# One hybrid layer on one core: attention's small products gathered at one point of each step, with the turning and the value products one step later

## The chip, the cores and the metric

The kernel is one program on one core of a Trainium2 chip. TensorE (PE) multiplies, VectorE (DVE), ScalarE (ACT) and GpSimd (POOL) work on rows, SyncE (SP) and ScalarE issue transfers. The metric is the device time of one execution in microseconds (us), the median of the runs.

## The reference

A decoder layer for 1024 tokens of width 1024: RMS norm, one wide input projection, sliding-window attention (window 128, 16 query heads, 4 key/value heads, a sink logit per head), a chunked mLSTM, two gated branch projections, an output projection and a final norm. What matters here is attention:

```
scores = einsum('bnqkgd,bnskd->bnkgqs', qb, kw) * (ATTN_HEAD_DIM ** -0.5)
allowed = (rel >= 0) & (rel < WINDOW) & (k_pos >= 0)
scores = where(allowed, scores, -inf)
probs = softmax(concatenate([scores, sink]))[..., :-1]
out = einsum('bnkgqs,bnskd->bnqkgd', probs, vw)
branch_a = einsum('bte,ed->btd', attn * silu(a_z), w_branch_attn)
```

Tokens are in 8 blocks of 128 (`n`), and each block of queries sees its own and the previous block of keys.

## The kernel before

The input projection runs as pairs of output tiles. A pair is seven products of 12 dense matmuls each (`PRODUCT` = 12, `PAIR` = 84), with 512 columns each, in the order 1, 6, 2, 7, 4, 5, 3, by `pairs(i0, lo, hi)`; all of them are recorded at L1036. Each product needs the high and the low part of a weight tile in a ring. SP loads the raw tile, ACT makes the high part (L1396), POOL makes the low part and the sums of tiles (L799, L794). ACT copies bank A away (L1435), DVE adds the other banks up (L2091 to L2115).

Attention's small operations are put in between these dense matmuls by position. There are four attention steps, one for each key/value head (`g` = 0 to 3; "group" below), and in each of them 3 * PAIR = 252 dense matmuls run. `attention_at(n, half)` gives the position in these 252 at which the program of an engine turns to block step `n`:

```
LEAD, TAIL = 12, 12
return LEAD + (3 * PAIR - LEAD - TAIL) * (2 * n + half) // (2 * NB + 2)
```

PE, ACT and DVE each walk through the block steps in their own queue. PE runs dense matmuls up to a position with `more(position)`; ACT and DVE do what belongs to the products that ended before it with `retire(position)`. In block step n of a group:

- PE at the first point runs `scores(n)` (L1123, q times k of 64 rows, two products side by side), which waits until DVE has `max_ready` for n-1. At the second point, some 12 to 13 dense matmuls later, it runs the value products of block n-2 (L1165, L1167, 64 output columns, two side by side) and then turns the probabilities of block n-1 (L1172).
- ACT copies the scores (L1596), waits for the row maximum, and takes the exponentials (L1599, L1601). For the first three blocks it also copies the attention output to `u_early` (L1609).
- DVE: `combine` (L2191 or L2194, then L2197 to L2203) merges two blocks of scores and makes the maximum, `select` (L2222, L2224) masks the turned probabilities, `gate` (L2236) multiplies the output by the gate, `normalise` (L2208 to L2214) scales the probabilities by the inverse of their sum. `silu` is L2230, and L2262 applies the gate to the three early blocks (in block step 5 of the last group, in 8 of the others). The order is combine(n), select(n-1), gate(n-2), normalise(n).

After the last group, ACT and DVE wait until all of `u_scratch` is stored (L1632, L2278) before the mLSTM part starts, because the store's source lies where they write next. ACT then makes the first taps of the convolution (L1713), small tables, and then the high parts for the first mLSTM pair; POOL follows with the low parts. At the start, ACT waits for a store of the values, loads `v_head` for the first group (L1493), and then makes the high parts for the next pair.

Tile sizes, transfers and buffers are not touched by the change. `probs` has two buffers; scores share two PSUM banks, turned probabilities have one and the value products one.

Of the kernel before, what the change touches and what calls it, by code (L numbers as in the profile page):

```python
# [9 lines left out]
ACT = mybir.ActivationFunctionType  # L10
# [3 lines left out]
P = 128  # L14
# [3 lines left out]
NB = T // P  # L18
# [36 lines left out]
PAIR = 7 * PRODUCT  # L55
# [1 line left out]
OPAIRS = NB // 2  # L57
BANK_A, BANK_B, BANK_C, BANK_D = 2, 3, 0, 1
EARLY = 3
LEAD, TAIL = 12, 12  # L60


def slot(t):
# [8 lines left out]
def until(eng, sem, value):  # L72

    if isinstance(value, int) and value <= 0:
        return
    eng.wait_ge(sem, value)
# [26 lines left out]

def attention_at(n, half):

    return LEAD + (3 * PAIR - LEAD - TAIL) * (2 * n + half) // (2 * NB + 2)


# [6 lines left out]
def build(nc, x, norm_w, w_in, b_in, sinks, conv_w, conv_b, mnorm_w, wba, wbm, w_out, fnorm_w, out):  # L115
    ctx = ExitStack()
    with ctx:
# [106 lines left out]
        u_early = at("u_early", M_AT, [P, 2, EARLY * P])  # L224
# [702 lines left out]
        def _(pe):  # L927
# [199 lines left out]
            def attention_step(g):  # L1127
                i0 = 1 + 3 * g
                done = [0]

                def more(hi):

                    pairs(i0, done[0], hi)
                    done[0] = hi

                for n in range(NB + 2):
                    more(attention_at(n, 0))
                    if n < NB:
                        if n == 0:
                            pe.wait_ge(k_in, 32 * (g + 1))  # L1140
                            pe.wait_ge(c11_out, i0)
                            pe.wait_ge(c12_out, i0)
                            if not later(g):
                                pe.wait_ge(g_ready, 1)
                        else:
                            pe.wait_ge(cur_copied, NB * g + n)
                            pe.wait_ge(max_ready, NB * g + n)
                        scores(n).then_inc(scores_done, 1)
                    if n <= NB:
                        more(attention_at(n, 1))  # L1150
                    if n >= 2:
                        m = n - 2
                        pe.wait_ge(pT_ready, NB * g + m + 1)
                        if m == 0:
                            pe.wait_ge(v_in, 16 * (g + 1))
                        if m == 0 and later(g):
                            pe.wait_ge(attn_gated, (NB - EARLY) * g)
                        if 1 <= m <= EARLY:
                            pe.wait_ge(attn_copied, EARLY * g + m)
                        if m > EARLY:  # L1160
                            pe.wait_ge(attn_gated, (NB - EARLY) * g + m - EARLY)
                        for r in range(2):
                            o = ps[64 * r:64 * r + 64, X[3], 0:2 * P]
                            heads = slice(2 * r, 2 * r + 2)
                            mm = nc.tensor.matmul(o, v_head[:, m, :], pT_cur[:, heads, :], start=True, stop=(m == 0))  # L1165
                            if m:
                                mm = nc.tensor.matmul(o, v_head[:, m - 1, :], pT_prev[:, heads, :], start=False, stop=True)  # L1167
                        mm.then_inc(pv_done, 1)
                    if 1 <= n <= NB:
                        pe.wait_ge(probs_ready, NB * g + n)  # L1170
                        for h in range(GR):
                            mm = nc.tensor.transpose(ps[:, X[2], h * P:(h + 1) * P], probs[(n - 1) % 2][:, h, :], ident[:])  # L1172
                        mm.then_inc(probs_turned, 1)
                more(3 * PAIR)

# [169 lines left out]
        def _(act):  # L1345
# [149 lines left out]
            def gate_tables():  # L1495
                act.wait_ge(g_turned, 1)
                A(gate_T[:].rearrange("p g h c -> p (g h c)"), ps[:, X[0], 0:2 * P], ACT.Copy).then_inc(g_ready, 1)

            def after(q, i, part, last=False):

                if q == 0:
                    keep_a(i, part)
                    high_4(i)
                if q == 1:
                    high_5(i)
                if q == 4 and not last:
                    high_1(i + 1)
                if q == 5 and not last:
                    high_6(i + 1)
                    high_2(i + 1)  # L1510
                if q == 6 and not last:
                    high_7(i + 1)
                    high_3(i + 1)
# [10 lines left out]
            act.drain()  # L1524
            load_k(0)
            gate_tables()
            act.wait_ge(v_out, 16 * 2)
            load_v(0)
            for q in range(2, 7):
                after(q, 0, None)  # L1530


            def attention_step(g):
# [33 lines left out]
                def retire(position):  # L1567

                    for q in range(done[0], position // PRODUCT):
                        if q < 7:  # L1570
                            after_z(q)
                        elif q < 14:
                            after_ga(q - 7)
                        else:
                            after_next(q - 14)
                    done[0] = max(done[0], position // PRODUCT)
# [9 lines left out]
                        act.wait_ge(z_used, 4 * g + m - 1)  # L1586
                    A(z_part[:, j, :], z_dest(j, h), ACT.Tanh, scale=0.5).then_inc(z_tanh, 1)

                for n in range(NB + 2):
                    retire(attention_at(n, 0))  # L1590
                    if n < NB:
                        pr = probs[n % 2]
                        act.wait_ge(scores_done, NB * g + n + 1)
                        if n >= 2:
                            act.wait_ge(probs_turned, NB * g + n - 1)
                        A(pr[:], both_blocks[:, :, 1, :], ACT.Copy).then_inc(cur_copied, 1)  # L1596
                        act.wait_ge(max_ready, NB * g + n + 1)
                        for h in range(GR):
                            A(pr[:, h, :], pr[:, h, :], ACT.Exp, scale=HD ** -0.5, bias=neg_max[:, h:h + 1],  # L1599
                              accum_out=row_sum[:, h:h + 1])  # L1600
                        A(sink_exp[:], sink_in[:], ACT.Exp).then_inc(exp_ready, 1)  # L1601
                    if n == NB and not final(g, KV):
                        load_k(g + 1)
                    if 2 <= n < EARLY + 2:
                        m = n - 2
                        act.wait_ge(pv_done, NB * g + m + 1)
                        if m == 0:
                            until(act, early_used, g)
                        A(u_early[:, :, m * P:(m + 1) * P], ps[:, X[3], 0:2 * P].rearrange("p (j n) -> p j n", j=2),  # L1609
                          ACT.Copy).then_inc(attn_copied, 1)  # L1610
                    if n <= NB:
                        retire(attention_at(n, 1))
                    if n in (3, 4):
                        for m in range(2):
                            tanh_z(2 * (n - 3) + m)
                    if n == (7 if final(g, KV) else 9):
                        act.wait_ge(u_half, g + 1)
                        act.dma_start(scr_u[ds(2 * g, 2)].rearrange("a p n -> p a n")[:, :, token_half(0)],
                                      silu_z[:, :, token_half(0)]).then_inc(u_half_out, 16)
# [373 lines left out]
        def _(dve):  # L1993
# [149 lines left out]
            def attention_step(g):  # L2143
# [91 lines left out]
                    z_m = silu_z[:, :, m * P:(m + 1) * P]  # L2235
                    return V.tensor_tensor(z_m, ps[:, X[3], 0:2 * P].rearrange("p (j n) -> p j n", j=2), z_m, ALU.mult)  # L2236

                for n in range(NB + 2):
                    retire(attention_at(n, 0))
                    if n < NB:  # L2240
                        combine(n)
                    if n <= NB:
                        retire(attention_at(n, 1))
                    if 1 <= n <= NB:
                        select(n - 1)
                    if n >= EARLY + 2:
                        gate(n - 2).then_inc(attn_gated, 1)
                    if n == NB + 1:
                        dve.drain()
                        dve.sem_inc(u_ready, 1)  # L2250
                    if n < NB:
                        normalise(n)
                    if n == 4:
                        silu(0)
                        silu(1)
                        dve.drain()
                    if n in (5, 7):
                        silu(2 if n == 5 else 3)
                        dve.drain()  # L2259
                    if n == (5 if final(g, KV) else 8):  # L2260
                        dve.wait_ge(attn_copied, EARLY * (g + 1))
                        V.tensor_tensor(silu_z[:, :, 0:EARLY * P], u_early[:], silu_z[:, :, 0:EARLY * P], ALU.mult)\  # L2262
                            .then_inc(early_used, 1)
                        dve.drain()
                        dve.sem_inc(u_half, 1)
# [403 lines left out]
```

## Time and the profile before

| | us |
|---|---|
| median of 3 runs | 1122.09 (1121.55 to 1122.24) |
| the profiled execution's own time | 1122.33 |
| span of the profiled execution | 1120.6 |

The profile is of one execution. Its span runs from the first to the last instruction; 1.7 us of the profiled time lie around it. The profiled time is 0.24 us above the median.

### The profile page before, as it was taken

What the parts mean: (1) busy time and instruction counts of PE and PEld (TensorE: products, weight loads), DVE (VectorE), ACT (ScalarE), POOL (GpSimd) and SP (SyncE); (2) the same over time, 40 slices, a digit from 0 to 9 for tenths busy, and PEclk for the clock granted to TensorE, in tenths of its full rate; (3) what the DMA queues carried; (4) which work ended last, traced back from release to release, by engine and by line L of the source; (5) the groups of instructions that cost most, each with busy time, mean ns of one, the idle gap of its engine ahead of it and who ended that gap; (6) DMA issues with size and microseconds to landing.
All of it is one profiled execution on the core that took longest, in us unless ns stands there. A gap on an engine that the chain in (4) does not pass through costs nothing.

```text
span 1120.6 us, 16419 instructions
## 1 busy us (share of the span) xinstructions
PE 1100.2 (98%) x5363; PEld 877.0 (78%) x5363; DVE 777.9 (69%) x1235; ACT 483.3 (43%) x1134; POOL 641.3 (57%) x441
## 2 busy tenths in 40 slices
PE   6999999999999999999999999999999999999997
PEld 5887777777777778888888888888887888788876
DVE  4966887887878887567756675669578312458897
ACT  7543443534434444454535364545455311131443
POOL 3577455465565469556955695659644434347440
PEclk9999999999999999999999999999999999999999
DMA  6244133142151141112311222122109433853423
GB/s 211 78 86 83 39 94 94 29 117 72 37 149 36 39 136 38 38 39 85 104 38 39 77 88 61 37 75 85 48 20 336 160 104 106 268 167 136 167 93 134
DMA packets 112804, 107.63 MB, mean 96 GB/s; under 512 B 7228, under 2 KB 96696, under 8 KB 111720
## 3 DMA queue, kind: packets, MB, share of 16 engines
q1 hardware_dynamic: 102760, 77.18, 23.2%
q10 hardware_dynamic: 9984, 29.69, 8.5%
q8 instruction: 33, 0.54, 0.2%
q14 instruction: 27, 0.22, 0.1%
HBM read 80.50 MB, written 26.35 MB: 95 GB/s over the span
## 4 chain that ended last, share of the span: by engine, by line
PE 79%; DVE 9%; ACT 4%; DVEq 3%; DMA 2%; issue 2%; ACTq 1%; SPq 0%; POOL 0%; POOLq 0%
PE ps L1036 50%; PE ps L1265 13%; PE ps L942 3%; PE ps L1123 2%; DMA w_raw<-in_w_branch_mlstm 1%; PE ps L1239 1%; PE ps L1223 1%; PE ps L1227 1%; PE ps L1236 1%; PE ps L1165 1%; DVE row_max L2197 1%; PE ps L1172 1%; DVEq L2259 1%; ACT ring_hi L1396 1%; DVE v L2427 1%
## 5 line engine op out<-in xcount | busy, mean ns | idle before, releaser
L799 POOL TENSOR_TENSOR ring_lo<-w,ring_hi 128x512 fp32r<-128x512 f32 x128 | 178.7, 1413 | 136.3 <-ACT ring_hi L1396 136.3
L799 POOL TENSOR_TENSOR ring_lo<-t,ring_hi 128x512 fp32r<-128x512 f32 x96 | 136.3, 1424 | 143.0 <-ACT ring_hi L1396 143.0
L1036 PE MATMUL ps<-s_hi,ring_hi 128*128 128x512 f32 x512 | 203.5, 397 | 0.0
L1036 PE MATMUL ps<-s_lo,ring_hi 128*128 128x512 f32 x512 | 202.6, 396 | 0.0
L1036 PE MATMUL ps<-s_hi,ring_lo 128*128 128x512 f32 x512 | 202.0, 395 | 0.0
L1036 PE MATMUL ps<-h_hi,ring_hi 128*128 128x512 f32 x384 | 152.1, 396 | 0.0
L1036 PE MATMUL ps<-h_hi,ring_lo 128*128 128x512 f32 x384 | 151.9, 396 | 0.0
L1036 PE MATMUL ps<-h_lo,ring_hi 128*128 128x512 f32 x384 | 151.4, 394 | 0.0
L1396 ACT ACTIVATE ring_hi<-w 128x512 fp32r<-128x512 f32 x128 | 75.6, 620 | 93.4 <-PE ps L1036 78.4
L1036 PEld LDWEIGHTS ps<-s_hi,ring_hi 128*128 128x128 f32 x512 | 96.2, 188 | 22.1 <-issue 3.0
L1036 PEld LDWEIGHTS ps<-s_hi,ring_lo 128*128 128x128 f32 x512 | 96.3, 188 | 21.8 <-issue 2.6
L1036 PEld LDWEIGHTS ps<-s_lo,ring_hi 128*128 128x128 f32 x512 | 96.3, 188 | 19.7 <-issue 1.3
L1599 ACT ACTIVATE probs<-probs,neg_max 128x128 f32<-128x128 f32 x128 | 49.9, 391 | 111.2 <-DVE neg_max L2203 111.2
L794 POOL TENSOR_TENSOR t<-w,t 128x512 f32<-128x512 f32 x64 | 94.4, 1475 | 5.1 <-issue 5.1
L782 POOL TENSOR_TENSOR w_hi<-w_raw,zero_col 128x1024 fp32r<-128x1024 f32 (+1 forms) x18 | 37.2, 2065 | 101.2 <-PE ps L1265 58.9
L1036 PEld LDWEIGHTS ps<-h_hi,ring_hi 128*128 128x128 f32 x384 | 72.2, 188 | 16.8 <-issue 1.3
L1036 PEld LDWEIGHTS ps<-h_hi,ring_lo 128*128 128x128 f32 x384 | 72.2, 188 | 15.4 <-issue 1.3
L1036 PEld LDWEIGHTS ps<-h_lo,ring_hi 128*128 128x128 f32 x384 | 72.2, 188 | 15.3 <-issue 1.3
L1396 ACT ACTIVATE ring_hi<-t 128x512 fp32r<-128x512 f32 x96 | 59.3, 623 | 53.8 <-PE ps L1036 46.6
L1265 PE MATMUL ps<-u_a,w_hi 128*128 128x512 f32 x256 | 79.1, 390 | 0.3 <-DVE u_a L2432 0.3
L1814 ACT ACTIVATE ev<-ev 128x1024 f32<-128x1024 f32 x16 | 17.0, 1062 | 110.5 <-DVE merged L2509 49.4
L1265 PE MATMUL ps<-u_m,w_hi 128*128 128x512 f32 x192 | 59.9, 393 | 0.4 <-POOL w_lo L784 0.4
(331 smaller groups left out, 2318.9 us busy)
## 6 DMA issues: line engine op xcount, KB each, us to landing
w<-in_w_in SPq DMA_DIRECT2D x128, 256.0 KB, 3.0
xs<-in_x SPq DMA_DIRECT2D x8, 512.0 KB, 8.3
ga_scratch<-ev ACTq DMA_DIRECT2D x4, 1024.0 KB, 4.8
u_scratch<-silu_z ACTq DMA_DIRECT2D x8, 512.0 KB, 3.4
gm_scratch<-ev ACTq DMA_DIRECT2D x4, 1024.0 KB, 4.8
w_raw<-in_w_branch_attn SPq DMA_DIRECT2D x8, 512.0 KB, 4.1
u_a_f<-u_scratch SPq DMA_DIRECT2D x4, 1024.0 KB, 8.2
ev<-ga_scratch ACTq DMA_DIRECT2D x8, 512.0 KB, 3.5
```

The lines of the kernel that those rows point to most:

```text
L782: nc.gpsimd.tensor_tensor(hi, src, zero_col[:].to_broadcast(list(src.shape)), ALU.add)
L794: return nc.gpsimd.tensor_tensor(flat(dst), flat(a), flat(b), op)
L799: return nc.gpsimd.tensor_tensor(flat(lo[:]), flat(raw_or_sum[:]), flat(hi[:]).bitcast(F32), ALU.subtract)
L942: mm = nc.tensor.matmul(ps[:, 2 * s + b, :], w[:, k, :], h[:, k % KH, :], start=(r == 0), stop=(r == KT * TERMS - 1))
L1036: mm = nc.tensor.matmul(ps[:, bank, :], w[:, k, :], h[:, k, :], start=(m == 0), stop=(m == PRODUCT - 1))
L1123: mm = nc.tensor.matmul(o, q_T[rows, j, n * P:(n + 1) * P], k_now[rows, first * P:(n + 1) * P], start=True, stop=True)
L1165: mm = nc.tensor.matmul(o, v_head[:, m, :], pT_cur[:, heads, :], start=True, stop=(m == 0))
L1172: mm = nc.tensor.transpose(ps[:, X[2], h * P:(h + 1) * P], probs[(n - 1) % 2][:, h, :], ident[:])
L1265: mm = nc.tensor.matmul(ps[:, 2 * s + b, :], w[:, k, :], part(k)[(0, 1, 0)[term]][:, token_half(b)], start=(r == 0), stop=(r == KT * TERMS ...
L1396: return A(ring_slot[0][:], raw_or_sum[:], ACT.Copy)
L1599: A(pr[:, h, :], pr[:, h, :], ACT.Exp, scale=HD ** -0.5, bias=neg_max[:, h:h + 1], accum_out=row_sum[:, h:h + 1])
L1814: A(ev[:, j, :], ev[:, j, :], ACT.Tanh, scale=0.5).then_inc(gate_tanh, 1)
```

## The change

PE has one point in each block step: scores(n), then the value products of block n-3, then the turning of block n-2. There are 11 block steps for each group in place of 10, and the last one is at position 252. `TAIL` grows from 12 to 20. DVE does normalise(n-1), gate(n-3), select(n-2) and then combine(n). ACT copies the early output before the scores of the step. At the start, ACT loads `v_head` after the high parts of the next pair.

```
-LEAD, TAIL = 12, 12
+LEAD, TAIL = 12, 20
 def attention_at(n, half):
+    if n == NB + 2:
+        return 3 * PAIR
...
 # TensorE
-                for n in range(NB + 2):
+                for n in range(NB + 3):
                     more(attention_at(n, 0))
...
                         scores(n).then_inc(scores_done, 1)
-                    if n <= NB:
-                        more(attention_at(n, 1))
-                    if n >= 2:
-                        m = n - 2
+                    if n >= 3:
+                        m = n - 3
...
-                    if 1 <= n <= NB:
-                        pe.wait_ge(probs_ready, NB * g + n)
+                    if 2 <= n <= NB + 1:
+                        pe.wait_ge(probs_ready, NB * g + n - 1)
...
 # ScalarE
             gate_tables()
+            for q in range(2, 7):
+                after(q, 0, None)
             act.wait_ge(v_out, 16 * 2)
             load_v(0)
-            for q in range(2, 7):
-                after(q, 0, None)
...
-                for n in range(NB + 2):
+                for n in range(NB + 3):
                     retire(attention_at(n, 0))
+                    if 3 <= n < EARLY + 3:
+                        m = n - 3
+                        act.wait_ge(pv_done, NB * g + m + 1)
+                        if m == 0:
+                            until(act, early_used, g)
+                        A(u_early[:, :, m * P:(m + 1) * P], ps[:, X[3], 0:2 * P].rearrange("p (j n) -> p j n", j=2),
+                          ACT.Copy).then_inc(attn_copied, 1)
                     if n < NB:
                         pr = probs[n % 2]
                         act.wait_ge(scores_done, NB * g + n + 1)
...
                         A(sink_exp[:], sink_in[:], ACT.Exp).then_inc(exp_ready, 1)
                     if n == NB and not final(g, KV):
                         load_k(g + 1)
-                    if 2 <= n < EARLY + 2:
-                        m = n - 2
...
 # VectorE
-                for n in range(NB + 2):
+                for n in range(NB + 3):
                     retire(attention_at(n, 0))
+                    if 1 <= n <= NB:
+                        normalise(n - 1)
+                    if n >= EARLY + 3:
+                        gate(n - 3).then_inc(attn_gated, 1)
+                    if n == NB + 2:
+                        dve.drain()
+                        dve.sem_inc(u_ready, 1)
+                    if 2 <= n <= NB + 1:
+                        select(n - 2)
                     if n < NB:
                         combine(n)
                     if n <= NB:
                         retire(attention_at(n, 1))
-                    if 1 <= n <= NB:
-                        select(n - 1)
-                    if n >= EARLY + 2:
-                        gate(n - 2).then_inc(attn_gated, 1)
-                    if n == NB + 1:
-                        dve.drain()
-                        dve.sem_inc(u_ready, 1)
-                    if n < NB:
-                        normalise(n)
```

## Rows read from the trace of the kernel before

**Rows 1.** The page: the span and the busy time of each engine.
```profile
span 1120.6 us, 16419 instructions
...
PE 1100.2 (98%) x5363; PEld 877.0 (78%) x5363; DVE 777.9 (69%) x1235; ACT 483.3 (43%) x1134; POOL 641.3 (57%) x441
```

**Rows 2.** Waits of PE in the attention stage (us in total, times, longest).
```profile
PE ps L1165 <- DVE silu_z L2236: 1.4, 1, 1.4
PE ps L1172 <- DVE probs L2214: 0.2, 1, 0.2
```

**Rows 3.** Timeline of PE in one block step (start us, us, engine, line).
```profile
286.71 0.39 PE L1036 MATMUL ps<-h_lo,ring_hi 128*128 128x512 f32 x1
287.03 1.13 PE L1123 MATMUL ps<-k_now,q_T 64*128 64x256 f32 x8
288.10 0.50 PE L1036 MATMUL ps<-h_hi,ring_lo 128*128 128x512 f32 x1
288.43 0.40 PE L1036 MATMUL ps<-h_hi,ring_hi 128*128 128x512 f32 x1
...
290.95 0.39 PE L1036 MATMUL ps<-s_hi,ring_lo 128*128 128x512 f32 x1
291.27 0.66 PE L1165 MATMUL ps<-pT_cur,v_head 128*64 128x256 f32 x4
...
292.29 0.66 PE L1172 MATMUL ps<-ident,probs 128*128 128x128 f32 x4
292.70 0.47 PE L1036 MATMUL ps<-s_hi,ring_hi 128*128 128x512 f32 x1
```

**Rows 4.** Timeline of DVE in block steps 5 and 6, last group.
```profile
381.05 0.16 DVE L2203 TENSOR_SCALAR neg_max<-row_max 128x4 f32<-128x4 f32 x1
...
381.78 0.68 DVE L2222 TENSOR_TENSOR pT_cur<-ps,cur_T 128x512 f32<-128x512 f32 x1
382.38 0.68 DVE L2224 TENSOR_TENSOR pT_prev<-ps,prev_T 128x512 f32<-128x512 f32 x1
...
384.03 1.40 DVE L2214 TENSOR_TENSOR probs<-probs,row_inv 128x512 f32<-128x512 f32 x1
385.35 1.77 DVE L2230 SCALAR_TENSOR_TENSOR silu_z<-z_part,silu_z 128x512 f32<-128x512 f32 x1
387.21 1.87 DVE L2262 TENSOR_TENSOR silu_z<-u_early,silu_z 128x768 f32<-128x768 f32 x1
...
390.79 0.74 DVE L2191 COPY_PREDICATED probs<-from_prev,ps 128x512 f32<-128x512 int8 x1 [0.21 <-issue]
...
392.68 0.16 DVE L2203 TENSOR_SCALAR neg_max<-row_max 128x4 f32<-128x4 f32 x1
```

**Rows 5.** One line's instructions: normalise's product (durations ns min/median/max).
```profile
L2214 DVE TENSOR_TENSOR probs<-probs,row_inv x32: 691/1417/1784, 103.4 to 404.1; 128x512 f32<-128x512 f32 x32
```

**Rows 6.** Timeline of ACT and PE's weight loads at the start of attention.
```profile
91.05 0.63 ACT L1396 ACTIVATE ring_hi<-w 128x512 fp32r<-128x512 f32 x1 [3.01 <-DMA v_scratch<-v_stage]
...
93.11 0.19 PEld L1036 LDWEIGHTS ps<-h_hi,ring_hi 128*128 128x128 f32 x1 [0.43 <-POOL ring_lo L799]
```

**Rows 7.** Timeline from attention's last value product to the second mLSTM pair.
```profile
411.92 0.50 PE L1036 MATMUL ps<-s_hi,ring_hi 128*128 128x512 f32 x1
...
413.32 0.38 ACTq L1624 DMA_DIRECT2D u_scratch<-silu_z  x1
...
414.98 0.75 DVE L2115 SCALAR_TENSOR_TENSOR raw<-ps,par,raw 128x512 f32<-128x512 f32 x1 [1.79 <-PE ps L1036]
...
416.38 1.25 ACT L1713 ACTIVATE conv_q<-raw,par 128x1024 f32<-128x1024 f32 x1 [0.71 <-DMA u_scratch<-silu_z]
...
420.77 4.05 POOL L799 TENSOR_TENSOR ring_lo<-t,ring_hi 128x512 fp32r<-128x512 f32 x2 [3.25 <-ACT ring_hi L1396]
...
431.49 2.29 POOL L799 TENSOR_TENSOR ring_lo<-w,ring_hi 128x512 fp32r<-128x512 f32 x1
...
433.83 0.19 PEld L1036 LDWEIGHTS ps<-h_hi,ring_hi 128*128 128x128 f32 x1 [0.27 <-POOL ring_lo L799]
```

More of the change, by code:

```diff
@@ L1168, in attention_step @@
                         mm.then_inc(pv_done, 1)
-                    if 1 <= n <= NB:
-                        pe.wait_ge(probs_ready, NB * g + n)
+                    if 2 <= n <= NB + 1:
+                        pe.wait_ge(probs_ready, NB * g + n - 1)
                         for h in range(GR):
-                            mm = nc.tensor.transpose(ps[:, X[2], h * P:(h + 1) * P], probs[(n - 1) % 2][:, h, :], ident[:])
+                            mm = nc.tensor.transpose(ps[:, X[2], h * P:(h + 1) * P], probs[n % 2][:, h, :], ident[:])
                         mm.then_inc(probs_turned, 1)
@@ L1603, in attention_step @@
                         load_k(g + 1)
-                    if 2 <= n < EARLY + 2:
-                        m = n - 2
[L1606 to L1610, printed above, removed]
                     if n <= NB:
```

## Prediction

> **What bounds the kernel now.** I read the page first: PE is busy for 1100.2 of the span's 1120.6 us [rows 1], so the end is set by PE's queue, and another engine counts only where it makes PE wait. The waits of PE over the attention stage come next: 1.4 us once, in front of the last value product of the last group, and 0.2 us once [rows 2]. So what can be won is mostly time in which PE counts as busy, and that is read from starts, not from busy time. The timeline of PE in one block step shows it [rows 3]: from the dense start at 288.43 to the one at 290.95 lie 11 intervals, 0.229 us each. That is the cadence, and every interval that is longer is the price of a switch between kinds of matmul. Last I read the timeline of DVE [rows 4], since DVE is the engine that PE's new order leans on, and the places at both ends of the stage where ACT and POOL feed PE [rows 6, 7].
>
> **What a stop costs PE.** A stop at the scores costs, beside their own streaming, 0.32 - 0.23 = 0.09 us in front (286.71 to 287.03) and 0.33 - 0.23 = 0.10 us behind them, where the second dense matmul after the stop comes late (288.10 to 288.43). A stop at the value products again has 0.09 us in front (290.95 to 291.27). The scores take 1.07 us to the next dense start, the value products 1.02, the turning 0.41 [rows 3].
>
> **Stops removed.** Before, a group has a stop for scores in block steps 0 to 7 (8), and one for the other products in steps 1 to 9 (9): 17. After, it has one in each of the steps 0 to 10: 11. So 6 for each group are gone, 24 in all. A merged stop loses the 0.10 behind the scores and the 0.09 in front of the value products. The step from scores to value products is in no trace; the nearest rows are the step from value products to the turning, which lies inside the 1.02 us, and the 0.09 in front of either group. I take it as no dearer than what the scores pay at their end now, already inside the 1.07. So 0.19 to 0.20 us for each, 24 x 0.20 = 4.8 us. Bounds: 1.2 us, if the new step costs another 0.15 us; 7.0 us, if it costs nothing at all and the groups overlap by another 0.09. I take 4.8, since the fronts at both kinds of group are alike.
>
> The Trainium skill ("TensorEngine Tiling (Array Packing)", Key Properties) says that changing the tiling mode, and not just the tile, drains the array. Scores run on half the rows and value products on half the columns, so by this rule their meeting is no cheaper than a return to the full array: the merged stop saves one change of mode of five, not two. The rows, with 0.09 us in front of either kind, agree.
>
> **The stall before the last value product.** The 1.4 us [rows 2] is PE in block step 9 of the last group, waiting for gate(6) on DVE. In the new order gate(6) stands at the front of DVE's step 9, and the value product that needs it comes at position 252, 20 dense matmuls (4.6 us) after PE's stop in step 9. This wait and the 0.2 us go: 1.6 us. What is late next is in the next parts.
>
> **The first load.** ACT waits 3.01 us for the store of the values before the high part at 91.05, and PE's weight load at 93.11 waits 0.43 us for POOL, which waited for ACT [rows 6]. With `load_v` behind the high parts this goes. PE itself loses less than its weight load: 0.3 us. `v_head` is needed only in block step 3. The other moved transfers: `load_v` for the next group comes after position 252, 85 dense matmuls before its use; the second store of `u_scratch` too, and for groups 0 to 2 DVE asks for it only at the fourth product after; both are hidden.
>
> **The new wait: scores behind combine.** Scores(n+1) need combine(n). Before, combine was first in DVE's step. Now it stands behind select(n-2), which needs the turning at the end of PE's stop. Count from the start of scores(n): turning done at 1.07 + 1.02 + 0.41 + about 0.1 = 2.6; select 0.68 + 0.68, say 1.35; combine 2.05 (390.79 to the end of neg_max at 392.84 [rows 4]): 6.05. The new period is 24 or 25 dense matmuls and the products, 5.5 or 5.7 + 1.07 + 1.02 + 0.41 + 0.09 + about 0.1 = 8.2 or 8.4. So 2.1 us are left when DVE comes in time. DVE must then do all the rest between combine and combine, and its work in a cycle is the same as before, only turned round. The longest such cycle is in rows 4: from the end of neg_max at 381.21 to 392.84, 11.63 us with hardly any idle time, because silu(2), L2262 and two dense results fall into it. Put into the new order: block step 5's combine ends at 6.05 or a little later (6.05 to 6.7), step 6's then at 6.05 + 11.63 - 8.17 = 9.5 (10.2), and the scores of step 7 are due at 8.4: a stall of 1.1 to 1.8 us. But three of the operations are lengthened: normalise 1.40 us where the least is 0.69 [rows 4, 5], silu 1.77, and L2262 1.87. These stretch when POOL works beside them, and the phase against POOL will be another; with all three short the stall is nought. I take 1.2 us (0 to 1.8). In groups 0 to 2, L2262 is not in this cycle: 11.63 - 1.87 = 9.8, so combine ends 0.1 to 0.8 us before the scores are due, and other cycles have more. I take nothing there.
>
> The Trainium skill ("SBUF — State Buffer", Who interferes with whom) has it that a DVE instruction with two SBUF inputs and a GpSimd instruction that reads SBUF lock each other out for a whole instruction. Operations with one input from PSUM, as L2222, stay at 0.68 in the rows, and those with two from SBUF stretch: the trace agrees.
>
> **The new wait at the end of attention.** ACT may not start the first tap until the last store of `u_scratch` has landed. Before, the store was issued at 413.32, ahead of the end of the last product (DVE took that result at 414.98), and ACT got through at 416.38, 3.06 us after the issue, having waited 0.71 us [rows 7]. Now the last value product stands after the last dense product. PE: 1.0 us for it; DVE: its c12 (0.75 us from 414.98), then the gate, half as wide as a select, about 0.4. The issue comes some 1.6 us after c12's start: 416.6, 3.3 us later against the dense products. Landing 3.06 later: 419.6 in place of 416.38, so ACT is 3.2 us late. What is queued behind: two taps, tables, then high_4 and high_5, for which POOL waited until 420.77; POOL then works through without a gap until the low part at 431.49, which ends at 433.78, and PE's first matmul of the next pair, at 433.83, waits for exactly this (0.27 us of weight load) [rows 7]. So there is no slack here at all. PE is itself 1.2 us later by the value product with its two switches (that time is only moved from position 240 to 252, not added). A stall of 3.2 - 1.2 = 2.0 us is left, less what POOL wins: its operation of 2.29 us is a lengthened one (DVE's taps run beside it), and DVE is delayed less than POOL, since two memsets (414.98 to the taps) fill its wait. I take 1.7 us (0.8 to 2.8).
>
> **Sum.** -4.8 - 1.6 - 0.3 + 1.2 + 1.7 = -3.8. The profiled execution's 1122.33 us become 1118.5. That execution is 0.24 us above the median of 1122.09; I predict 1118.5, 0.32% under the median. A difference within 0.2% (2.2 us) is about what a measurement here can't tell from no change.
>
> **Rivals.**
> - *A. The two new waits come in full, and more* (the skew of DVE costs in all groups). In groups 0 to 2 the slack is only 0.1 to 0.8 us; with another 0.3 us of stretching, each of the three groups loses some 0.5 us, the last one 1.8, and the end 2.8: -6.7 + 1.5 + 1.8 + 2.8 = -0.6, 1121.7. For it: the median of normalise is 1.417 us, so stretching is the rule [rows 5]. Against it: rows 4 have it stretched already. Chance 0.18.
> - *B. DVE becomes the bound; slower.* Place: the wait of the scores for combine, in all 28 steps that have a successor. The loop scores, value product, turning, select, combine takes 6.05 us of 8.2. It decides from the point where a cycle of DVE is longer than 8.2 us on average. From rows 4, without L2262 and with silu and normalise short, a cycle is 11.6 - 1.9 - 1.1 - 0.7 = 7.9 in a step with silu; so it needs 0.3 us more. If every step were 0.35 us over the period, 28 x 0.35 = 10: -6.7 + 10 + 1.7 = +5, 1127. Against it: half of the steps have no silu, so 0.7 us less. Chance 0.10.
> - *C. The merged stop saves next to nothing* (the step from scores to value products costs 0.15 us or more): -1.2 - 1.9 + 2.9 = -0.2, 1122.1. Chance 0.10.
> - *D. The waits don't come:* the phase against POOL is kind, and the end costs 0.8: -6.7 + 0.8 = -5.9, 1116.4. Chance 0.20.
> - *The forecast,* 1117.3 to 1120.0: chance 0.42.
>
> **Range and chances.** Two in ten are left out if the range goes from 1115.8 (below D by the bound of the switches) to 1122.2 (A and C in, B out). Faster by over 0.2% means under 1119.85: the forecast but for its edge (0.40), D (0.20), a third of A (0.06): 0.66. Within 0.2%: the rest of A (0.10), the edge, C: 0.22. Slower: B and the worst of C: 0.12.
>
> **What would show it.** In the new profile, the starts from scores to value product should be 1.05 to 1.1 us apart, and the merged stop 2.5 us long. PE should wait in front of the scores of step 7 of the last group (releaser neg_max, L2203 before) by 0 to 1.8 us, and nowhere else for DVE. The idle time in front of the first tap should be some 3 to 4 us with the store as releaser, and PE should stand 1 to 3 us at the first product of the pair after, for POOL. The wait for gate(6) and the one at 93.11 should be gone. I am wrong if PE waits for neg_max in many steps (B), if the scores' end to value product's start is over 0.2 us (C), or if the mLSTM part, which nothing here touches, moves by over 1 us.

## The result and the profile after

The changed kernel takes 1135.65 us in the median of 4 runs (1135.07 to 1137.49), the kernel before 1122.16 (the three runs of before and one more). The ratio is 1.0123, with a 95% interval of 1.0106 to 1.0141: slower by 1.2%. The forecast was 1118.5, in a range of 1115.8 to 1122.2. The span of the profiled execution is 1133.6 us, 13.0 longer than [rows 1].

The page of the changed kernel, its first lines. PE's busy time is 1.5 us under that in [rows 1]; all of the growth is time in which PE stands still.

```profile
span 1133.6 us, 16419 instructions
...
PE 1098.7 (97%) x5363; PEld 880.9 (78%) x5363; DVE 781.1 (69%) x1235; ACT 482.4 (43%) x1134; POOL 639.6 (56%) x441
```

The waits of PE in the changed kernel, longest first (us in total, times, longest). The first line has no counterpart in [rows 2]; it is the scores standing for combine's maximum. Both waits of [rows 2] are gone. The third line is the stall at the second mLSTM pair. The second is in the opening, as before.

```profile
PE ps L1125 <- DVE neg_max L2203: 14.5, 11, 2.3
PE ps L954 <- DVE xs L2008: 7.9, 2, 7.5
PE ps L1038 <- POOL ring_lo L801: 1.4, 1, 1.4
```

The timeline of PE over one merged stop (block step 6 of the third group; start in us first) answers to [rows 3]. Scores to value products 1.06 us, these to the turning 1.02, the turning to a dense matmul 0.41: the stop is 2.49 us long.

```profile
308.93 0.39 PE L1038 MATMUL ps<-s_lo,ring_hi 128*128 128x512 f32 x1
309.25 1.14 PE L1125 MATMUL ps<-k_now,q_T 64*128 64x256 f32 x8
310.31 0.66 PE L1165 MATMUL ps<-pT_cur,v_head 128*64 128x256 f32 x4
310.79 0.61 PE L1167 MATMUL ps<-pT_prev,v_head 128*64 128x256 f32 x4
311.33 0.66 PE L1172 MATMUL ps<-ident,probs 128*128 128x128 f32 x4
311.74 0.48 PE L1038 MATMUL ps<-s_hi,ring_lo 128*128 128x512 f32 x1
```

The 11 waits stand in three places. In front of the scores of block step 5 it is 2.19, 2.26, 2.27 and 2.21 us in the four groups; in front of step 4 it is 0.54, 0.58, 0.59 and 0.91; in front of step 7 it is 0.98, 0.98 and 0.96 in the second, third and last group. The timeline of ACT in the changed kernel, third group, around block step 4, shows what ACT does once it has the maximum of step 3: exponentials for 1.7 us, and only then the copy of bank A (L1435).

```profile
290.32 0.40 ACT L1606 ACTIVATE probs<-probs,neg_max 128x128 f32<-128x128 f32 x1 [4.64 <-DVE neg_max L2203]
...
291.87 0.19 ACT L1608 ACTIVATE sink_exp<-sink_in 128x4 f32<-128x4 f32 x1
291.97 0.57 ACT L1435 ACTIVATE ev<-ps 128x512 f32<-128x512 f32 x1
```

The timeline of DVE over the same stretch. After neg_max at 290.13 (step 3) comes at once the dense result L2091, which adds bank B to that copy. DVE idles 2.29 us for it. Then normalise, select and combine follow without another wait, three of their operations lengthened, that is, longer than the same operation is elsewhere (L2208 1.09 us, L2214 1.79, L2200 1.15), and neg_max of step 4 ends at 300.97.

```profile
290.13 0.16 DVE L2203 TENSOR_SCALAR neg_max<-row_max 128x4 f32<-128x4 f32 x1
292.57 0.69 DVE L2091 TENSOR_TENSOR ev<-ps,ev 128x512 f32<-128x512 f32 x1 [2.29 <-ACT ev L1435]
293.36 1.09 DVE L2208 TENSOR_TENSOR row_inv<-row_sum,sink_exp 128x4 f32<-128x4 f32 x1
...
295.02 1.79 DVE L2214 TENSOR_TENSOR probs<-probs,row_inv 128x512 f32<-128x512 f32 x1
296.74 0.68 DVE L2222 TENSOR_TENSOR pT_cur<-ps,cur_T 128x512 f32<-128x512 f32 x1
...
297.94 0.72 DVE L2191 COPY_PREDICATED probs<-from_prev,ps 128x512 f32<-128x512 int8 x1
...
299.50 1.15 DVE L2200 SCALAR_TENSOR_TENSOR row_max<-row_max,sink_tab 128x4 f32<-128x4 f32 x1
...
300.81 0.16 DVE L2203 TENSOR_SCALAR neg_max<-row_max 128x4 f32<-128x4 f32 x1
```

The lengthened operations lie beside POOL's. Here is the POOL operation that runs beside L2200; L2200, on four columns, starts at 299.50 and ends with it, at 300.65.

```profile
299.38 1.26 POOL L796 TENSOR_TENSOR w<-w,w 128x512 f32<-128x512 f32 x1
```

In the kernel before, the same stretch of DVE's timeline (third group, from neg_max of step 3 to neg_max of step 4) has L2091 behind normalise, where the copy has been made for 0.6 us:

```profile
284.43 0.16 DVE L2203 TENSOR_SCALAR neg_max<-row_max 128x4 f32<-128x4 f32 x1
...
286.40 0.16 DVE L2208 TENSOR_TENSOR row_inv<-row_sum,sink_exp 128x4 f32<-128x4 f32 x1 [0.62 <-ACT sink_exp L1601]
...
287.75 0.68 DVE L2091 TENSOR_TENSOR ev<-ps,ev 128x512 f32<-128x512 f32 x1
290.11 0.75 DVE L2191 COPY_PREDICATED probs<-from_prev,ps 128x512 f32<-128x512 int8 x1 [1.68 <-ACT probs L1596]
...
292.58 0.16 DVE L2203 TENSOR_SCALAR neg_max<-row_max 128x4 f32<-128x4 f32 x1
```

Two things have changed, and they are about equally large. The cycle took 8.15 us before (284.59 to 292.74) and takes 10.68 now (290.29 to 300.97). The idle time is the same, 2.3 us, but before, 1.68 us of it were DVE waiting for ACT's copy of the next scores, at a place where PE waited for nothing; now all of it is spent ahead of work that the next scores need. And the time in which DVE works grew from 5.85 to 8.39 us with the same kinds of operations, by lengthening alone: L2208 was at 0.16 before and L2200 at 0.72, and the product of normalise at 0.69 (287.14).

PE's timeline in the changed kernel has the scores of step 4 at 290.43 and those of step 5 at 301.12, 10.7 us on, where 8.4 were due.

```profile
290.43 1.13 PE L1125 MATMUL ps<-k_now,q_T 64*128 64x256 f32 x8 [0.59 <-DVE neg_max L2203]
...
301.12 1.13 PE L1125 MATMUL ps<-k_now,q_T 64*128 64x256 f32 x8 [2.27 <-DVE neg_max L2203]
```

Two of these waits cost more than themselves. The windows of the first group (us of the window, busy us of PE, PEld, DVE, ACT, POOL with counts, then the granted clock) show full speed up to 134.0 and 0.72 in the six us behind; within them, 136 to 139 is at 0.50, that is at 1.2 and not 2.4 GHz. PE had stood 2.19 us just before (scores at 135.29). In the last group it is the same from 383 to 389.

```profile
120.00:134.00 14.00, 12.55 (x64) 9.34 (x62) 10.61 (x16) 5.17 (x16) 10.13 (x9) 1.00 0.22 57
134.00:140.00 6.00, 4.71 (x23) 2.87 (x24) 5.14 (x12) 3.46 (x13) 0.81 (x1) 0.72 0.01 4
...
136.00:139.00 3.00, 3.00 (x15) 1.23 (x12) 2.59 (x7) 2.03 (x9) 0.00 (x0) 0.50 0.02 5
...
383.00:389.00 6.00, 4.96 (x24) 3.28 (x25) 5.27 (x13) 3.76 (x13) 0.56 (x1) 0.72 0.01 3
```

A mean of 0.72 over 6 us is a loss of 0.28 x 6 = 1.7 us of PE's work, 3.4 us for both. The account of the span is then: waits for neg_max +14.5, clock +3.4, mLSTM start +1.4, waits of before gone -1.9 (1.6, and for the first load the 0.3 of the prediction, which no run measures by itself); that is +17.4. Measured are +13.0, so about 4.4 us are left for the merged stops. The rows give them directly: before, the two stops take 0.32 + 1.07 + 0.33 us and 0.32 + 1.02 + 0.41, the merged stop 0.32 + 1.06 + 1.02 + 0.41 with two dense intervals of 0.23 more. That is 0.20 us for each, 4.8 for 24.

### The profile page after: what moved, and what is told of

Its sections match the earlier page's. It is cut to its first block, busy times and chain, and to the rows that moved or that the text cites. A ratio compares the mean times of both kernels' runs of the same rounds, so it can differ in the third digit from the quotient of the medians.

```text
span 1133.6 us, 16419 instructions
## 1 busy us (share of the span) xinstructions
PE 1098.7 (97%) x5363; PEld 880.9 (78%) x5363; DVE 781.1 (69%) x1235; ACT 482.4 (43%) x1134; POOL 639.6 (56%) x441
## 4 chain that ended last, share of the span: by engine, by line
PE 56%; DVE 4%; DMA 2%; DVEq 1%; ACT 1%; issue 1%; POOL 1%; POOLq 1%; ACTq 0%; SPq 0%
PE ps L1038 35%; PE ps L1265 13%; DMA w_raw<-in_w_branch_mlstm 1%; PE ps L1239 1%; PE ps L1223 1%; PE ps L1227 1%; PE ps L1236 1%; DVE v L2427 1%; PE ps L1192 1%; PE ps L1247 1%; DVE u_a L2432 1%; DVEq L2196 0%; PE ps L1221 0%; PE ps L1222 0%; PE ps L1224 0%
## 5 line engine op out<-in xcount | busy, mean ns | idle before, releaser
L1038 PEld LDWEIGHTS ps<-h_hi,ring_lo 128*128 128x128 f32 x384 | 72.3, 188 | 14.5
```

Of the source, the lines that this page charges most:

```text
L1038: mm = nc.tensor.matmul(ps[:, bank, :], w[:, k, :], h[:, k, :], start=(m == 0), stop=(m == PRODUCT - 1))
```

## The experiments

Theory 1: with combine last in DVE's step, what comes next on DVE waits for ACT's copy, which stands behind the exponentials that this combine releases. Theory 2: select in front of combine makes one chain of scores, value products, turning, select and combine. Theory 3: DVE has too much work for the shorter step, in any order. The kernel before had a median of 1123.4 to 1123.5 on the chips of these runs, so the ratios, or the distances from it, are what is compared.

**The first load alone.** The kernel before with this:

```
             gate_tables()
+            for q in range(2, 7):
+                after(q, 0, None)
             act.wait_ge(v_out, 16 * 2)
             load_v(0)
-            for q in range(2, 7):
-                after(q, 0, None)
```

> The kernel before with one part of the change alone: the first load of v_head stands behind ScalarE's high parts. By my step in the prediction this takes away the wait of PE's weight load at 93.11 us (0.43 us) and gives 0.2 to 0.3 us; a rival says that the wait is hidden and gives 0.0.

1122.16 us, ratio 0.9989 (0.9979 to 0.9998). The sign is as expected; the size, 0.0 to 0.2%, is no finer than that. The medians differ by 1.3 us, and two later runs show how it can be more than 0.3: they leave the first load where it was before, and in their profiled executions ACT waits 4.64 and 4.39 us for the store of the values, where it was 3.01, and PE itself stands 1.60 and 1.36 us. These lines are of the run with the gathering alone, below.

```profile
92.50 0.63 ACT L1394 ACTIVATE ring_hi<-w 128x512 fp32r<-128x512 f32 x1 [4.64 <-DMA v_scratch<-v_stage]
...
94.53 0.50 PE L1036 MATMUL ps<-h_hi,ring_hi 128*128 128x512 f32 x1 [1.60 <-POOL ring_lo L799]
```

So what this part of the change gives differs from execution to execution, with the time that this store takes.

**Positions as before.** `LEAD, TAIL = 12, 12` in the changed kernel.

> The changed kernel with TAIL 12 as before, so the block steps lie 25 or 26 dense matmuls apart in place of 24 or 25. If the positions of the steps against the products cause the loss, PE's waits for neg_max (14.5 us) go and the time is about 1121. If it is the order on the engines, each wait gets shorter only by what the longer step gives (0.2 us each, 2 to 3 us in all) and the time is about 1132.

1130.94 us, ratio 1.0069 (1.0052 to 1.0085); 10.1 us of waits for neg_max in 8 places. The positions are not the cause of most of it. In the profiled execution the waits in front of step 4 are gone and those in front of step 7 are 0.5 us, but in front of step 5 still 1.9 to 2.2; the clock fell once in place of twice. With 0.7 us of new waits for pT_prev, that is 5.4 us less, most of what the 0.5% are.

**Combine ahead of gate and select.** On DVE, in the changed kernel:

```
                     if 1 <= n <= NB:
                         normalise(n - 1)
+                    if n < NB:
+                        combine(n)
                     if n >= EARLY + 3:
                         gate(n - 3).then_inc(attn_gated, 1)
...
                         select(n - 2)
-                    if n < NB:
-                        combine(n)
```

> The changed kernel with one turn on VectorE: combine(n) stands before gate(n-3) and select(n-2). Theory 1 (combine last in the step: what follows it, a dense result, waits for ScalarE's copy of bank A, and that stands behind the exponentials which this combine releases, so VectorE idles 2.3 us) and theory 2 (select in front of combine is simply too much for the slack) both say that most of the 14.5 us go, 1 to 3 us left, and the time is 1118.5 to 1122. Theory 3 (VectorE has too much work in a step, whatever its order) says that the waits stay at 10 us or more and the time over 1130.

1133.75 us, ratio 1.0088 (1.0071 to 1.0105). All three expectations were off in part: the time did not fall as theories 1 and 2 said, and the 10.9 us of waits were what theory 3 said. The timeline of DVE, third group, block step 4, shows why theory 1 is not refuted by it. The dense result and normalise still stand ahead of combine; DVE does select (289.02) while ACT is at the exponentials, and still idles 1.09 us. My expectation overlooked this. And what the order gave in idle time was lost by lengthening: four operations from there to neg_max were lengthened (three in the changed kernel), and the one at 298.33 took 1.14 us on four columns. The cycle is 10.44 us long in place of 10.68. The waits are 3.6 us less than in the changed kernel, but the clock fell behind four of them, in place of two.

```profile
288.95 0.16 DVE L2203 TENSOR_SCALAR neg_max<-row_max 128x4 f32<-128x4 f32 x1
289.02 0.69 DVE L2222 TENSOR_TENSOR pT_cur<-ps,cur_T 128x512 f32<-128x512 f32 x1
...
291.40 0.69 DVE L2091 TENSOR_TENSOR ev<-ps,ev 128x512 f32<-128x512 f32 x1 [1.09 <-ACT ev L1435]
...
298.33 1.14 DVE L2202 TENSOR_TENSOR sink_in<-sink_tab,row_max 128x4 f32<-128x4 f32 x1
299.39 0.16 DVE L2203 TENSOR_SCALAR neg_max<-row_max 128x4 f32<-128x4 f32 x1
```

**ACT's results ahead of the exponentials.** In the changed kernel:

```
                         A(pr[:], both_blocks[:, :, 1, :], ACT.Copy).then_inc(cur_copied, 1)
+                        retire(attention_at(n, 1))
                         act.wait_ge(max_ready, NB * g + n + 1)
```

> The changed kernel with one turn on ScalarE: the copies and high parts of the products that end by the second position are made while it waits for the row maximum, ahead of the exponentials, not behind them. Theory 1 (VectorE idles for ScalarE's copy of bank A) says that the wait of the scores of block step 5 (2.3 us in each group) goes, and the clock drop that follows it, so the time is about 1123 to 1125, with about 1 us left in front of step 7. Theory 2 (select in front of combine) and theory 3 (too much work) say that 12 us or more of waits stay and the time is over 1132.

1126.8 us, ratio 1.0025 (1.0016 to 1.0035): some 10 us less than the changed kernel by one line (that one was 13.5 us over the kernel before in the medians, this one 3.4). The four waits in front of step 5 are gone. The timeline of DVE in the same block step shows L2092 (the line of L2091) behind neg_max without an idle time. It is theory 1 that this run bears out, but 7.9 us of waits are left, more than it allowed: 1.3 us in front of step 7 in three groups and 2.50 in the last, which a stretch at half clock follows, and 0.3 to 0.6 in front of step 3 or 4.

The same lines show that the turn did more than take the wait for the copy away. The cycle to neg_max of step 4 is 6.91 us long in place of 10.68, 3.8 us less. Of these only 1.16 are idle time (1.13 us are left, now for the exponentials of the sink). The rest, some 2.6 us, is lengthening that is gone: L2209 is at 0.16 us (it was 1.09), L2215 at 0.69 (1.79), L2201 at 0.48 (1.15). POOL's work follows ACT's high parts, so with ACT's order POOL's timing against DVE changed too. Theory 1 had only the idle time.

```profile
285.02 0.16 DVE L2204 TENSOR_SCALAR neg_max<-row_max 128x4 f32<-128x4 f32 x1
285.18 0.69 DVE L2092 TENSOR_TENSOR ev<-ps,ev 128x512 f32<-128x512 f32 x1
287.00 0.16 DVE L2209 TENSOR_TENSOR row_inv<-row_sum,sink_exp 128x4 f32<-128x4 f32 x1 [1.13 <-ACT sink_exp L1609]
...
287.73 0.69 DVE L2215 TENSOR_TENSOR probs<-probs,row_inv 128x512 f32<-128x512 f32 x1
...
291.30 0.48 DVE L2201 SCALAR_TENSOR_TENSOR row_max<-row_max,sink_tab 128x4 f32<-128x4 f32 x1
...
291.93 0.16 DVE L2204 TENSOR_SCALAR neg_max<-row_max 128x4 f32<-128x4 f32 x1
```

**Scores last in the stop.** In PE's part of the changed kernel, the block from `if n < NB:` to `scores(n).then_inc(scores_done, 1)` goes behind the turning:

```
                 for n in range(NB + 3):
                     more(attention_at(n, 0))
-                    if n < NB:
...
                         mm.then_inc(probs_turned, 1)
+                    if n < NB:
...
+                        scores(n).then_inc(scores_done, 1)
                 more(3 * PAIR)
```

> The changed kernel with one turn on TensorE: in its stop it runs the value products, then the turning, and the scores last. The turned probabilities are then there 1.1 us earlier against the scores, so select and combine no longer follow the scores one after the other. Theory 2 (the chain scores, value products, turning, select, combine eats the slack) says that the waits for neg_max fall from 14.5 us to under 3 us, and the time is 1119 to 1121. Theory 1 (VectorE idles for ScalarE's copy) says that the idle time of 2.3 us stays in block step 4 and about 1 us of it in each group is still seen by TensorE: 1123 to 1125. Theory 3 (too much work on VectorE in a step) says that 10 us or more of waits stay.

1131.02 us, ratio 1.0064 (1.0039 to 1.0089). The waits for neg_max are down to 4.8 us, but 4.4 us came up in front of the value products, for pT_prev: DVE is late all the same, and now its select is seen. The clock is at 0.999, with no drop. Theory 1's idle time is there as before (2.29 us in the second and in the third group), and so is the length of this cycle, 10.69 us. Neither theory alone explains it.

**Both turns.**

> Both turns: scores last on TensorE, and ScalarE makes copies and high parts ahead of the exponentials. Theories 1 and 2 say that no wait for neg_max is left (under 1 us), no clock drop, and the time is 3 to 4 us under the kernel before, 1.4 us of stall at the first mLSTM pair included. Theory 3 says that waits of 5 us or more stay and it is slower than before.

1121.43 us, ratio 0.9983 (0.9973 to 0.9992). The waits of PE in the attention stage are 0.4 us for neg_max and 0.2 us for pT_prev, with the same instructions on DVE. So they fit into a step in this order, and theory 3, which said that no order would do, falls. Its time on them is not the same: DVE is busy for 770.2 us in all, in the changed kernel for 781.1. The time is only 0.2% under the kernel before, not the 3 to 4 us that were expected. The timeline of PE shows a step that costs more than I had put: the turning takes 0.59 us up to the scores, where it takes 0.41 up to a dense matmul. The stop is 2.68 us long.

```profile
291.81 0.66 PE L1154 MATMUL ps<-pT_cur,v_head 128*64 128x256 f32 x4
292.30 0.61 PE L1156 MATMUL ps<-pT_prev,v_head 128*64 128x256 f32 x4
292.83 0.66 PE L1161 MATMUL ps<-ident,probs 128*128 128x128 f32 x4
293.42 1.13 PE L1125 MATMUL ps<-k_now,q_T 64*128 64x256 f32 x8
294.49 0.50 PE L1038 MATMUL ps<-h_hi,ring_lo 128*128 128x512 f32 x1
```

**And the last stop at position 240.** `return 3 * PAIR - PRODUCT` in `attention_at`.

> As the run with both turns, and the last stop of a group at position 240 in place of 252. If the stall of TensorE at the first product of the second mLSTM pair (1.4 us, for GpSimd's low part) comes from the late store of u_scratch, it goes, with ScalarE's wait of 4.4 us for that store down to 1.5 us or less, and the time is 1.4 us under the run with both turns. If it comes from elsewhere, nothing moves.

1119.94 us, ratio 0.9960 (0.9947 to 0.9973), 1.5 us less. PE's wait of 1.4 us for ring_lo is gone, and ACT waits 0.19 us for the store, where it was 4.37 us in the changed kernel and in the run with both turns. The first line is of this run, the second of the changed kernel.

```profile
413.43 1.25 ACT L1714 ACTIVATE conv_q<-raw,par 128x1024 f32<-128x1024 f32 x1 [0.19 <-DMA u_scratch<-silu_z]
```

```profile
429.93 1.25 ACT L1713 ACTIVATE conv_q<-raw,par 128x1024 f32<-128x1024 f32 x1 [4.37 <-DMA u_scratch<-silu_z]
```

**The gathering alone.** The kernel before without `more(attention_at(n, 1))` on PE, so that value products of n-2 and turning of n-1 follow the scores at once.

> The kernel before with the gathering alone: value products of block n-2 and turning of block n-1 stand behind the scores at the first point, no block later than before; VectorE and ScalarE as before. It saves 7 stops in each group, 28 in all: -5.6 us at 0.20 us each. What stands against it: the turning now needs normalise of the block step just before, which ended 9.4 to 11.5 us after the scores of its step, so 1 to 3 us into the next; the turning starts 2.1 us into it, and waits of up to 1 us come in some steps. I expect 3 to 6 us of waits for probs, and a time between 1119 and 1124; theory 3 (too much work on VectorE) would have 10 us or more.

1129.97 us, ratio 1.0052 (1.0037 to 1.0068), slower. PE waits 12.8 us for normalise, in 13 places. I had expected at most 6 us. (The 1.60 us at 94.53, shown above, come on top.) Gathering at one point without moving the turning one step later loses more than the stops give, with DVE and ACT in the order of before; it was not tried with ACT's turn.

**Value products, scores, turning.** As the run with the last stop at 240, with the scores between the other two.

> The fastest so far (ScalarE's turn, last stop at 240) with the stop in the order value products, scores, turning. In the run with the scores last, the turning took 0.59 us to the start of the scores, against 0.41 us to a dense matmul when it stands last, and the stop 2.68 us against 2.50 us. If that step is what ate the saving of the merged stops, this order gives it back: 0.18 us in each of 24 merged stops, 4.3 us, less the slack that combine loses (1.0 us of it with the scores 1.0 us earlier in the stop), which should cost under 1 us of waits. I expect 1116.5 to 1118 on the scale where the kernel before is 1122.1. If the switches are not what was missing, it stays at the ratio 0.996.

1117.72 us, ratio 0.9952 (0.9939 to 0.9966). The stop is 2.50 us long (289.72 to 292.22 in the timeline of PE), the waits are 2.2 and 0.6 us. It is the fastest version, faster than either kernel by its interval. Against the run before it the medians differ by 2.2 us, which is 4.3 us won by the order less 2.2 us of added waits; the intervals of the two ratios overlap, but the times don't (1117.36 to 1118.03 against 1119.27 to 1120.42, with the same kernel before at 1123.45 and 1123.5 beside them).

```profile
289.72 0.66 PE L1154 MATMUL ps<-pT_cur,v_head 128*64 128x256 f32 x4
290.20 0.61 PE L1156 MATMUL ps<-pT_prev,v_head 128*64 128x256 f32 x4
290.74 1.13 PE L1125 MATMUL ps<-k_now,q_T 64*128 64x256 f32 x8
291.81 0.66 PE L1172 MATMUL ps<-ident,probs 128*128 128x128 f32 x4
292.22 0.48 PE L1038 MATMUL ps<-h_hi,ring_lo 128*128 128x512 f32 x1
```

**ACT's turn on the kernel before.**

> The kernel before with ScalarE's turn alone (copies and high parts ahead of the exponentials). Before the change VectorE had select, gate and normalise to do while ScalarE was at the exponentials, and TensorE waited 1.6 us in all of attention. If ScalarE's turn is worth something only with combine last in VectorE's step, this gives 0 to 1.5 us (the wait of 1.4 us in the last group may go). If it is a gain in itself, it gives more than 2 us.

1121.54 us, ratio 0.9985 (0.9976 to 0.9994); PE waits 0.3 us for DVE in attention in place of 1.6 (and 1.36 us for POOL at its start, see the first run). So of these two kernels the turn is worth its 10 us only in the one with combine last in DVE's step.

## Why the prediction was wrong

- **Stops, -4.8 us: right.** The rows give 0.20 us for each of 24, the account of the span leaves 4.4 us, and the merged stop is 2.49 us long. The step from scores to value products, unseen before, costs no more than the others, as taken. The experiments add that this is no rule for every pair: turning to scores costs 0.18 us more. The prediction also says that the merged stop saves one change of mode of five, not two. Counted in its own rows, the changes are four before (the turning and the dense matmuls both use the full array) and three after, and what is saved is the price of two steps of 0.09 to 0.10 us, not of one.
- **Waits that go, -1.6 and -0.3 us: right for the first; the second has the right sign, and its size is open.** Neither is in the trace after. The first load alone gave 1.3 us in the medians, with an interval of 0.0 to 0.2%, and other executions show PE standing up to 1.60 us at this place; the one execution that the 0.3 was read from shows 0.43 us of weight load only.
- **The end of attention, +1.7 us: right.** 1.4 us measured, by the named path, and the run with the last stop at 240 took just this away. Inside it two sizes were off and made up for each other in part. ACT was late by 3.7 us and not 3.2 (its wait for the store is 4.37 us against 0.71): the issue came when it was expected, but the store took 3.47 us to let ACT through and not 3.06. And the POOL operation that took 2.29 us took 1.26.
- **Scores behind combine, +1.2 us: wrong, and this is the step that failed.** It measured 14.5 us, and 3.4 us of clock behind it. At the place that the prediction named, step 7 of the last group, the wait is 0.96 us and within its 0 to 1.8; the rest is at ten places at which it took nothing, step 7 of the second and third group among them (0.98 us each). The sentence at fault is that DVE's "work in a cycle is the same as before, only turned round", used as if the length of a cycle could be carried over with it. Work can be turned round; waits can't, and here the durations of the work didn't stay either. Before, combine(3) was followed by select and normalise and only then by L2091, and ACT had time for its exponentials (1.7 us) and its copy of bank A (0.57 us). With combine last, DVE reaches a dense result that needs this copy straight after neg_max, and the two engines work one after the other: 2.29 us idle in block step 4. [Rows 4], the only cycle I looked at closely, has no such result. Beside that, the lengthening in this cycle grew by 2.5 us. The cycle is then 10.68 us long where the period is 8.2 to 8.4. I took the cycle with the most work (step 5 to 6) for the worst one and wrote that "other cycles have more" slack. The worst one is the next to it, from neg_max of step 3 to that of step 4, with less work and one wait. (The chain from the scores adds up to 6.0 us and not 6.05, which changes nothing.)
- What the single runs say of the cause: measured by the distance of the medians from the kernel before (13.5 us for the changed kernel), ACT's turn alone takes 10.1 us off (3.4 us left), the scores last take 6.0 off (7.5 left), and both together 15.6 (2.1 under it). The turns share their waits: each one alone still leaves 8 to 9 us of them, both leave 0.6. So it is shown that the 14.5 us come from the order of work on ACT and PE against DVE's new order. ACT's turn removes the idle time for the copy and most of the lengthening in the same cycle together, so how the 14.5 us divide among the copy, the lengthening and the chain over select is open.
- **Stretching of DVE by POOL** was rightly seen as a cost that can't be foretold. Its share was larger than the prediction and theory 1 allowed: in block step 4 even operations on four columns take 1.09 and 1.15 us in place of 0.16, and in that cycle lengthening grew by 2.5 us, about as much as DVE's idle time for the copy is long (2.29). With ACT's turn most of it is gone from there. No run changed the lengthening and nothing else, so how much of the 14.5 us it is stays open.
- **Rival B was the right one, by place and by mechanism in part** (scores wait for combine; 1127 forecast, 1135.65 measured), at a chance of 0.10. Its condition, 28 waits from a cycle that is too long on average, did not hold: there are 11 waits.
- The clock was in none of the cases. A wait of 2.2 us of PE brought a stretch at 0.50 of full speed in the profiled execution twice; four waits of about this length occurred.

## What to carry to other kernels

When the order of work on one engine is turned round, list for each item what it waits for and where that stands in the other engine's queue; a cycle's length carries over only if each such wait still has other work in front of it. Durations that depend on what another engine does at the same time don't carry over either. An item that releases another engine should not be followed at once by an item that needs what this engine does next: put independent work between them, or let the other engine do its independent work ahead of the wait. Here one line on ScalarE and one move on TensorE turned a loss of 1.2% into a gain of 0.2%, and with the last stop and the order in the stop, into one of 0.5%.

## What was not expected of the hardware

- A pause of PE of 2.19 us was followed by some 3.4 us at half clock (a mean of 0.72 over 6 us) in the first group and likewise in the last; the pauses of 2.3 us in the second and third group of the same execution were not. So a pause may cost 1.7 us more than itself, or not. Over the attention stages of the profiled executions here there are 15 pauses of 1.8 to 2.5 us, and nine of them were followed by such a stretch; the shortest of these nine was 1.81 us long, the longest of the other six 2.27.
- The order of kinds within a stop matters: the turning took 0.41 us to a dense matmul and 0.59 us to the scores, the scores 1.06 or 1.07 us to the value products, to the turning and to a dense matmul alike.
- Lengthening of DVE beside POOL is largest in proportion for small operations: one on four columns took 1.15 us in place of 0.16, about as long as the whole POOL operation beside it (1.26 us). It moves with ACT's order, because POOL's low parts wait for ACT's high parts: DVE's busy time was 781.1 us in the changed kernel and 772.6 with one line moved on ACT.
